# Head mean squares of a hybrid decoder layer: two fp32r matmuls on split squares in place of one fp32 matmul

## The chip, the cores and the metric

One core of one Trainium2 chip runs the kernel. The metric is device time in microseconds (us). Three runs of the kernel before took 942.68, 943.15 and 943.49 us; the median is 943.15.

## What is computed

The reference is one layer of a decoder trunk for 512 prompt rows and 8 sample rows, width 1024. The part that matters here is the RMS norm of each head's output, in the two branches (HGRN2: 8 heads of width 64; retention: 4 heads of width 128):

```python
def _head_rmsnorm(o, n_heads, g):
    b, l, w = o.shape
    oh = o.reshape(b, l, n_heads, w // n_heads)
    oh = oh * lax.rsqrt(jnp.mean(oh * oh, axis=-1, keepdims=True) + EPS)
    return oh.reshape(b, l, w) * g.astype(jnp.float32)

a_hg = _head_rmsnorm(_merge_heads(o_hg), HG_HEADS, g_hg_out) * silu(hg)   # branch A
a_r  = _head_rmsnorm(_merge_heads(o_r), RET_HEADS, g_ret_out) * silu(rg)  # branch B
```

Everything else of the layer (input projection, the two recurrences, the branch and output projections, ConvFFN, per-layer embedding, final norm) is unchanged.

## The kernel before

Activations are kept transposed: channels on the 128 partitions, the 520 rows (512 prompt, 8 sample) along the free dimension. The projections are done in sections named A, V, B, C, D, E, F, G, H. Each section is a run of units; one unit is a stripe of weights of 128 output columns. A unit's raw weights arrive by a DMA on SP's queue (`load`, L396), ScalarE (ACT) makes their high part in the narrow 4-byte kind fp32r (`hi`, L831), VectorE (DVE) the low part (`lo`, L1168), and TensorE (PE) multiplies (`product`, L485): for each 128 channels, high by high, high by low and low by high, each in two halves of 260 columns. There are two weight slots, so the high and low part of unit k+2 are made when the products of unit k are done.

The recurrences run beside the projections, by hand placed into the order of each engine. Both go over the prompt in four chunks of 128 rows.

Section B (`Fori` over four chunks, L597): between the units B0 to B3 of retention's q, k, v and gate, the PE computes one HGRN2 chunk. Its scores go by seven levels (`scores`, L568, matmul L586 and L582), the DVE merges each level's scores into `sfull` (`merge`, L1276), GpSimd (POOL) makes the decayed queries and keys of the levels (`next_level`, L1598 to L1602), ACT pads the queries (`pad_queries`, L922). Then come the chunk's outputs in the PSUM bank `ob` (L617, L622), the state's update in the bank `mb` (L626), half of unit B3, and in `head_squares` the head mean squares: ACT squares `ob` into `sq` (L968), the PE multiplies `sq` by the block constant `blk64` into `mb` (L635), ACT takes the root into `rs` (L970), the DVE inverts it and gates the output (`gate_outputs`, L1289 to L1293). Before L635 the PE also waits until the DVE has added the state's update out of `mb` (L1336).

Section C (`Fori` over four chunks, L652): between the units C0 to C3 the PE computes one retention chunk. ACT squares `ob` at L1021, the PE multiplies by `ones128` at L684 in the middle of unit C2, ACT takes the root at L1023. The DVE adds the state's update out of `mb` at L1369, scales the sample state `rsm` at L1373, and gates.

```python
pe.wait_ge(sq_ready, it + 1)
wait_misc(M_B, 2, it, 4)                    # until L1336 is done
pe.matmul(mb[:], blk64, sq[:], start=True, stop=True).then_inc(misc_full, 1)
```

`sq`, `blk64` and `ones128` are fp32. Such a matmul leaves two records in the profile, one for each of its two passes over the 512 columns.

Of the kernel before, what the change touches and what calls it, by code (L numbers as in the profile page):

```python
# [62 lines left out]
def hybrid_layer(nc, x_prompt, x_sample, state_hgrn, state_ret, state_conv, p_prompt, p_sample,  # L63
# [30 lines left out]
    class Region:  # L94
# [3 lines left out]
        def __call__(self, name, shape, dt=fp):  # L98
# [9 lines left out]
    raw = [r(f"raw{i}", [128, WMAX]) for i in range(2)]  # L108
    whi = [r(f"whi{i}", [128, WMAX], fr) for i in range(2)]
    wlo = [r(f"wlo{i}", [128, WMAX], fr) for i in range(2)]  # L110
    r = Region(33792, 49152)
    NCST = consts.shape[1]
    CST0 = r.at
# [45 lines left out]
    tl = [None] + [r(f"tl{i}", [128, 4, CH >> i]) for i in range(1, LV + 1)]  # L159
    sbd = r("sbd", [128, 4, 128])  # L160
    qz = r("qz", [128, 2, NS])
    sq = r("sq", [128, 512])
    rs = r("rs", [128, 512])
    vb = r("vb", [128, 1024])
    ks8 = r("ks8", [128, 8])
# [20 lines left out]
    zq = [at(f"zq{i}", [128, 4, 2, CH // 2], o)  # L186
          for i, o in enumerate((T0 + 10400, r.at + 2048, r.at - 2048, T0 + 3 * TT * 4))]
    rsm = r("rsm", [128, 8, 128])

    r = Region(G0, 212832)  # L190
    xtok = at("xtok", [128, 5, DM], G1)
# [52 lines left out]
    with ctx:  # L244
        def sem(name):
            return ctx.enter_context(nc.semaphore(name))
# [43 lines left out]
        staged = sem("staged")  # L290
        outer_ready = sem("outer_ready")
        vst_ready = sem("vst_ready")
        sq_ready = sem("sq_ready")
        o_free = sem("o_free")
        a_done = sem("a_done")
# [158 lines left out]
        def _(pe):  # L454
# [142 lines left out]
            with pe.Fori(0, 4) as it:  # L597

                def first_scores():
                    pe.wait_ge(v_taken, it * 2 + 9)  # L600
                    scores(0, it)

                halves(0, it, first_scores)
                scores(1, it)
                halves(1, it, lambda: scores(2, it))
                scores(3, it)
                pe.wait_ge(prep, it * 8 + 8)
                wait_misc(M_B, 0, it, 4)
                for c in range(4):
                    mm = pe.transpose(mb[:, c * 128:(c + 1) * 128], lk[3][:, c, :], ident)  # L610
                mm.then_inc(misc_full, 1)

                product("B", 2, it, 0, 2, C8, 0, xah, xal)

                pe.wait_ge(o_free, it + 1)
                for c in range(4):
                    pe.matmul(ob[:, c * 128:(c + 1) * 128], sbd[:, c, :], lq[3][:, c, :], start=c == 0, stop=False)  # L617
                pe.wait_ge(merged, it * MERGES + (MERGES + 1))
                pe.wait_ge(vst_ready, it + 1)
                wait_misc(M_B, 1, it, 4)  # L620
                for h in range(8):
                    mm = pe.matmul(ob[64 * (h % 2):64 * (h % 2) + 64, (h // 2) * 128:(h // 2 + 1) * 128],  # L622
                                   vst[:, h * 64:(h + 1) * 64], sfull[:, h, :], start=False, stop=h >= 6)
                mm.then_inc(o_ready, 1)
                for h in range(8):
                    mm = pe.matmul(mb[64 * (h % 2):64 * (h % 2) + 64, (h // 2) * 64:(h // 2 + 1) * 64],  # L626
                                   khat[:, h * 64:(h + 1) * 64], vst[:, h * 64:(h + 1) * 64],
                                   start=True, stop=True)
                mm.then_inc(misc_full, 1)

                def head_squares():

                    pe.wait_ge(sq_ready, it + 1)
                    wait_misc(M_B, 2, it, 4)
                    pe.matmul(mb[:], blk64, sq[:], start=True, stop=True).then_inc(misc_full, 1)  # L635
                    pe.wait_ge(acc_free[0], tidx("B", 2, it) + 1)
                    v_transposes()

                halves(3, it, head_squares)

                wait_misc(M_B, 3, it, 4)
                pe.wait_ge(smp_staged, it + 1)
                pe.wait_ge(ss_ready, it + 1)
                taken()
                for b in range(NS):
                    for h2 in range(2):
                        mm = pe.matmul(mb[64 * h2:64 * h2 + 64, b:b + 1], ss[:, b, :], qz[:, h2, b:b + 1],
                                       start=True, stop=True)
                mm.then_inc(misc_full, 1)
            pe.wait_ge(v_taken, 17)  # L650

            with pe.Fori(0, 4) as it:  # L652
                product("C", 0, it, 0, 0, C8, 0, xah, xal)
                pe.wait_ge(staged, it * 2 + 1)
                pe.wait_ge(vst_ready, it + 5)
                wait_level(L_C, 0, it, 2)
                for h in range(4):
                    mm = pe.matmul(level(0)[:, h * 128:(h + 1) * 128], kst[:, h, :], qst[:, h, :],
                                   start=True, stop=True)
                mm.then_inc(lv_full, 1)  # L660
                wait_level(L_C, 1, it, 2)
                for h in range(4):
                    mm = pe.transpose(level(1)[:, h * 128:(h + 1) * 128], kst[:, h, :], ident)
                mm.then_inc(lv_full, 1)
                product("C", 1, it, 1, 1, C8, 0, xah, xal)
                for b in range(2):
                    pe.wait_ge(lv_free[b], it + L_C // 2 + 1)
                pe.wait_ge(o_free, it + 5)
                pe.wait_ge(staged, it * 2 + 2)
                for h in range(4):  # L670
                    out = ob[:, h * 128:(h + 1) * 128]
                    pe.matmul(out, vst[:, h * 128:(h + 1) * 128], prb[:, h, :], start=True, stop=False)
                    mm = pe.matmul(out, rst[:, h, :], qd[:, h, :], start=False, stop=True)
                mm.then_inc(ret_o, 1)
                wait_misc(M_C, 0, it, 4)
                for h in range(4):
                    mm = pe.matmul(mb[:, h * 128:(h + 1) * 128], ktk[:, h * 128:(h + 1) * 128],
                                   vst[:, h * 128:(h + 1) * 128], start=True, stop=True)
                mm.then_inc(misc_full, 1)

                product("C", 2, it, 0, 2, range(4), 0, xah, xal, last=False)
                pe.wait_ge(sq_ready, it + 5)
                wait_misc(M_C, 1, it, 4)
                pe.matmul(mb[:], ones128[:], sq[:], start=True, stop=True).then_inc(misc_full, 1)  # L684
                product("C", 2, it, 0, 2, range(4, 8), 4, xah, xal, first=False, wait_unit=False)
                wait_misc(M_C, 2, it, 4)
                pe.wait_ge(smp_staged, it + 5)
                pe.wait_ge(rsm_ready, it + 1)
                for b in range(NS):
                    mm = pe.matmul(mb[:, b:b + 1], rsm[:, b, :], qs8[:, b:b + 1], start=True, stop=True)  # L690
                mm.then_inc(misc_full, 1)

                product("C", 3, it, 1, 3, range(5), 0, xah, xal, last=False)

                pe.wait_ge(smp_sq, it + 1)
                wait_misc(M_C, 3, it, 4)
                pe.matmul(mb[:, 0:8], blk64, sqs[:, 0:8], start=True, stop=True)
                pe.matmul(mb[:, 8:16], ones128[:], sqs[:, 8:16], start=True, stop=True).then_inc(misc_full, 1)
                product("C", 3, it, 1, 3, range(5, 8), 5, xah, xal, first=False, wait_unit=False)
# [116 lines left out]
        def _(act):  # L816
# [93 lines left out]
            def pad_queries(l, it):  # L910
# [11 lines left out]
                    ins = act.activation(dst, src, ACT.Copy)  # L922
                ins.then_inc(zq_ready, 1)

            act.wait_ge(v_taken, 9)
            act.dma_start(vs_dram[0], v8h[:]).then_inc(vs_stored, 16)
            act.wait_ge(set_up, 7)
# [3 lines left out]
            def hgrn_chunk(it, last=False):  # L931
# [33 lines left out]
                act.dma_start(hg_sample[0].rearrange("b (c two) k v -> (two k) c b v", two=2)[:, it], ss[:])\  # L965
                    .then_inc(ss_stored, 16)
                act.wait_ge(o_ready, it + 1)
                act.activation(sq[:], ob[:], ACT.Square).then_inc(sq_ready, 1)  # L968
                act.wait_ge(misc_full, it * 4 + (M_B + 3))
                act.activation(rs[:], mb[:], ACT.Sqrt, bias=eps[:]).then_inc(misc_free, 1)  # L970
                act.wait_ge(v_full, it * 2 + 10)
# [20 lines left out]
            with act.Fori(0, 4) as it:  # L992
# [8 lines left out]
                for k in range(4):  # L1001
# [16 lines left out]
                                      .broadcast_to([128, NS, 128])).then_inc(vb_loaded, 32)  # L1018
                    if k == 1:
                        act.wait_ge(ret_o, it + 1)  # L1020
                        act.activation(sq[:], ob[:], ACT.Square).then_inc(sq_ready, 1)  # L1021
                        act.wait_ge(misc_full, it * 4 + (M_C + 2))
                        act.activation(rs[:], mb[:], ACT.Sqrt, bias=eps[:]).then_inc(misc_free, 1)  # L1023
                        act.wait_ge(rsm_ready, it + 1)
# [127 lines left out]
        def _(dve):  # L1152
# [134 lines left out]
            def gate_outputs(gate, it, n, per=1):  # L1287
# [4 lines left out]
                dve.wait_ge(o_free, it + (n + 2))  # L1292
                dve.tensor_tensor(m4(ot[:]), m4(ot[:]), chunk(gate, it), MUL).then_inc(a_done, 1)  # L1293

            def branch_lo(t_lo, t_hi, it, n):

                dve.wait_ge(ah_hi, it + (n + 1))
# [2 lines left out]
            with dve.Fori(0, 4) as it:  # L1300
# [33 lines left out]
                for h2 in range(2):  # L1334
                    mine = slice(64 * h2, 64 * h2 + 64)
                    grown = dve.tensor_tensor(state(h2), state(h2),  # L1336
                                              mb[mine, 0:256].rearrange("p (c v) -> p c v", c=4), ADD)
                grown.then_inc(misc_free, 1)
                dve.wait_ge(misc_free, it * 4 + (M_B + 3))
                gate_outputs(ghg, it, 0)  # L1340

# [12 lines left out]
            with dve.Fori(0, 4) as it:  # L1354
# [12 lines left out]
                step(dve.tensor_tensor(rst[:], rst[:], g128.unsqueeze(2).broadcast_to([128, 4, 128]), MUL))  # L1367
                dve.wait_ge(misc_full, it * 4 + (M_C + 1))
                dve.tensor_tensor(rst[:], rst[:], m4(mb[:]), ADD).then_inc(misc_free, 1)  # L1369
                dve.wait_ge(rsm_loaded, it * 16 + 16)  # L1370
                dve.wait_ge(outer_ready, it + 5)
                grown = rsm[:].rearrange("p b v -> p (b v)")
# [400 lines left out]
```

## Time and profile before

| | |
|---|---|
| median of three runs | 943.15 us |
| profiled execution, its own time | 943.24 us |
| its span, first to last instruction | 941.5 us |
| PE busy | 918.6 us, 98% |
| DVE busy | 524.1 us, 56% |
| ACT busy | 388.6 us, 41% |
| POOL busy | 235.7 us, 25% |
| granted clock of TensorE | 0.996 |
| section B's chunk loop | about 121 to 264 us |
| section C's chunk loop | about 264 to 388 us |

The profile is of one execution. A row of the timeline gives the start, the length, the engine, the line, the operation, output and inputs, and how many instructions were merged into it; in brackets stand the engine's idle time before it and what ended it. A queue row (ACTq, SPq) is a DMA's issue. PEld is TensorE's weight load, which overlaps the matmul before.

### The profile page before, as it was taken

Reading aid. Unit: us, or ns where it says so; the run is one execution under the profiler, and the core shown is the slowest. Engines: PE = TensorE matmul, PEld = TensorE weight load, DVE = VectorE, ACT = ScalarE, POOL = GpSimd, SP = SyncE. Lnnn points to the kernel's source line nnn. Section 1 sums busy time; section 2 is a strip of 40 time slices with the busy share of each in tenths; the row PEclk is TensorE's granted clock in tenths of the full one; section 3 lists DMA queues with packets and bytes.
Section 4 is the critical chain, followed back from the end, with each engine's and each line's share of the span. In section 5 each row is a group of like instructions: output and inputs, shape, how many; then the busy total and the mean of one; then the engine's idle time right before and its main releaser. Section 6 shows DMA issues by size and latency. Waiting matters only on the chain. (4 is left out here: it accounts for less than half of the span.)

```text
span 941.5 us, 21025 instructions
## 1 busy us (share of the span) xinstructions
PE 918.6 (98%) x7964; PEld 904.2 (96%) x7964; DVE 524.1 (56%) x612; ACT 388.6 (41%) x518; POOL 235.7 (25%) x289
## 2 busy tenths in 40 slices
PE   7999999999999999999999999999999999999996
PEld 6999989999999999999999999999999999999995
DVE  5432258878655654666566556666655443434643
ACT  6322355465444544423345444444443221223433
POOL 0007057867410101001641111111111031212341
PEclk9999999999999999999999999999999999999998
DMA  6233533323334344533323333333233433332212
GB/s 221 70 90 90 180 92 90 85 71 89 89 112 119 106 125 142 177 116 98 91 68 104 96 91 89 89 89 89 89 89 100 121 93 92 92 90 63 85 56 91
DMA packets 176472, 94.74 MB, mean 101 GB/s; under 512 B 17888, under 2 KB 174960, under 8 KB 176016
## 3 DMA queue, kind: packets, MB, share of 16 engines
q1 hardware_dynamic: 149698, 80.61, 28.8%
q10 hardware_dynamic: 26736, 13.60, 5.1%
q8 instruction: 26, 0.43, 0.2%
q14 instruction: 12, 0.10, 0.0%
HBM read 86.25 MB, written 8.03 MB: 100 GB/s over the span
## 5 line engine op out<-in xcount | busy, mean ns | idle before, releaser
L1168 DVE TENSOR_TENSOR wlo<-raw,whi 128x1024 fp32r<-128x1024 f32 (+2 forms) x132 | 195.8, 1483 | 174.4 <-ACT whi L831 174.4
L831 ACT ACTIVATE whi<-raw 128x1024 fp32r<-128x1024 f32 (+2 forms) x132 | 146.7, 1111 | 353.4 <-PE acc L485 352.0
L485 PE MATMUL acc<-xah,whi 128*128 128x260 f32 x896 | 187.7, 291 | 0.0
L485 PE MATMUL acc<-xah,wlo 128*128 128x260 f32 x896 | 180.8, 283 | 0.0
L485 PE MATMUL acc<-xal,whi 128*128 128x260 f32 x896 | 180.5, 283 | 0.0
L485 PE MATMUL acc<-xbh,whi 128*128 128x260 f32 x816 | 165.3, 284 | 0.8 <-issue 0.8
L485 PE MATMUL acc<-xbh,wlo 128*128 128x260 f32 x816 | 164.4, 283 | 0.0
L485 PE MATMUL acc<-xbl,whi 128*128 128x260 f32 x816 | 164.2, 283 | 0.0
L485 PEld LDWEIGHTS acc<-xah,whi 128*128 128x128 f32 x896 | 138.6, 189 | 3.3 <-issue 1.9
L485 PEld LDWEIGHTS acc<-xal,whi 128*128 128x128 f32 x896 | 138.6, 189 | 0.0
L485 PEld LDWEIGHTS acc<-xah,wlo 128*128 128x128 f32 x896 | 138.4, 189 | 0.0
L485 PEld LDWEIGHTS acc<-xbh,whi 128*128 128x128 f32 x816 | 125.8, 188 | 1.1 <-issue 1.0
L485 PEld LDWEIGHTS acc<-xbh,wlo 128*128 128x128 f32 x816 | 125.8, 188 | 0.0
L485 PEld LDWEIGHTS acc<-xbl,whi 128*128 128x128 f32 x816 | 125.5, 188 | 0.0
L485 PE MATMUL acc<-ach,whi 128*128 128x260 f32 x352 | 71.2, 283 | 0.0
L485 PE MATMUL acc<-ach,wlo 128*128 128x260 f32 x352 | 70.8, 282 | 0.0
L485 PE MATMUL acc<-acl,whi 128*128 128x260 f32 x352 | 70.6, 282 | 0.0
L1670 POOL TENSOR_TENSOR sqt<-hT 128x520 f32 x23 | 35.5, 1543 | 125.6 <-DVE hT L1423 101.3
L1690 POOL TENSOR_TENSOR gg<-gg,cv 128x520 f32<-128x520 f32 x22 | 28.9, 1314 | 118.1 <-DVE gg L1484 115.3
L485 PEld LDWEIGHTS acc<-acl,whi 128*128 128x128 f32 x352 | 54.3, 188 | 0.0
L485 PEld LDWEIGHTS acc<-ach,whi 128*128 128x128 f32 x352 | 54.2, 188 | 0.1
L485 PEld LDWEIGHTS acc<-ach,wlo 128*128 128x128 f32 x352 | 54.2, 188 | 0.0
(286 smaller groups left out, 1194.7 us busy)
## 6 DMA issues: line engine op xcount, KB each, us to landing
raw<-in_w_in SPq DMA_DIRECT2D x96, 256.0 KB, 3.2
raw<-in_w_up SPq DMA_DIRECT2D x88, 256.0 KB, 3.1
raw<-in_w_down SPq DMA_DIRECT2D x16, 384.0 KB, 3.2
raw<-in_w_down SPq DMA_DIRECT2D x16, 320.0 KB, 3.7
raw<-in_w_out SPq DMA_DIRECT2D x16, 256.0 KB, 3.0
raw<-in_w_ple_gate SPq DMA_DIRECT2D x8, 512.0 KB, 3.7
x_transposed<-xstg SPq DMA_DIRECT2D x1, 2080.0 KB, 7.7
hT<-x_transposed ACTq DMA_DIRECT2D x1, 2080.0 KB, 8.3
```

The lines of the kernel that those rows point to most:

```text
L485: mm = pe.matmul(sums[:, b, 0:HT], wt[slot][:, w], xx[:, c, b * HT:(b + 1) * HT], start=first and i == 0 and q == 0, stop=last and i == n ...
L831: act.activation(whi[k % 2][:, 0:n], raw[k % 2][:, 0:n], ACT.Copy).then_inc(hi_ready, 1)
L1168: dve.tensor_tensor(wlo[k % 2][:, 0:n], raw[k % 2][:, 0:n], whi[k % 2][:, 0:n].bitcast(fp), SUB).then_inc(lo_ready, 1)
L1670: step(pool.tensor_tensor(sqt[:], hT[:, j, :], hT[:, j, :], MUL))
L1690: pool.tensor_tensor(gg[:], gg[:], cv[:], MUL).then_inc(act_ready, 1)
```

## The change

The constants `blk64` and `ones128` get copies in the kind fp32r, `blk64r` and `ones128r`, made once by ACT and placed in the part of the first high-weight slot that sections B and C leave unused. After the square, ACT copies `sq` to `sqh` in fp32r (the high part). The DVE then takes `sq - sqh` in place into `sql`, also fp32r (`squares_lo`), right after the state's update. The PE waits for that and does two accumulating fp32r matmuls of 512 columns, on `sqh` and `sql`, in place of the one fp32 matmul. This happens in the four chunks of section B and in the four of section C. The small matmuls on the sample rows' squares (L697, L698) stay as they were.

```diff
@@ tensor, section B, head_squares (L635)
-                    pe.matmul(mb[:], blk64, sq[:], start=True, stop=True).then_inc(misc_full, 1)
+                    pe.wait_ge(sums_ready, 1)
+                    pe.matmul(mb[:], blk64r[:], sqh[:], start=True, stop=False)
+                    pe.matmul(mb[:], blk64r[:], sql[:], start=False, stop=True).then_inc(misc_full, 1)
@@ tensor, section C (L684)
-                pe.matmul(mb[:], ones128[:], sq[:], start=True, stop=True).then_inc(misc_full, 1)
+                pe.matmul(mb[:], ones128r[:], sqh[:], start=True, stop=False)
+                pe.matmul(mb[:], ones128r[:], sql[:], start=False, stop=True).then_inc(misc_full, 1)
@@ scalar, once, ahead of L925
+            act.activation(blk64r[:], blk64, ACT.Copy)
+            act.activation(ones128r[:], ones128[:], ACT.Copy).then_inc(sums_ready, 1)
@@ scalar, section B (L968); section C (L1021) in the same way with it + 5
-                act.activation(sq[:], ob[:], ACT.Square).then_inc(sq_ready, 1)
+                act.activation(sq[:], ob[:], ACT.Square).then_inc(sq_full, 1)
+                act.wait_ge(sq_full, it + 1)
+                taken()
+                act.activation(sqh[:], sq[:], ACT.Copy).then_inc(sq_hi, 1)
@@ vector
+            def squares_lo(it, n):
+                dve.wait_ge(sq_hi, it + (n + 1))
+                dve.tensor_tensor(sql[:], sq[:], sqh[:].bitcast(fp), SUB).then_inc(sq_ready, 1)
@@ vector, section B, after the state's update (L1336)
                 grown.then_inc(misc_free, 1)
+                squares_lo(it, 0)
                 dve.wait_ge(misc_free, it * 4 + (M_B + 3))
@@ vector, section C, after the state's update (L1369)
                 dve.tensor_tensor(rst[:], rst[:], m4(mb[:]), ADD).then_inc(misc_free, 1)
+                squares_lo(it, 4)
                 dve.wait_ge(rsm_loaded, it * 16 + 16)
```

## Rows read from the trace of the kernel before

**Rows 1.** The page: span and busy time.
```profile
span 941.5 us, 21025 instructions
PE 918.6 (98%) x7964; PEld 904.2 (96%) x7964; DVE 524.1 (56%) x612; ACT 388.6 (41%) x518; POOL 235.7 (25%) x289
```

**Rows 2.** Waits of PE: line, releaser, total us, times, longest.
```profile
PE lvb L586 <- DVE sfull L1276: 2.1, 3, 0.8
```

**Rows 3.** The tile `sq`: its matmuls, duration ns min/median/max, first and last start.
```profile
L635 PE MATMUL mb<-sq,cst x8: 592/593/697, 152.0 to 259.0; 128*128 128x512 f32 x8
L684 PE MATMUL mb<-sq,ones x8: 591/592/592, 282.4 to 373.1; 128*128 128x512 f32 x8
```

**Rows 4.** Timeline of PEld in section C, around L684: start, length.
```profile
282.30 0.31 PEld L684 LDWEIGHTS mb<-sq,ones 128*128 128x128 f32 x2
282.85 0.19 PEld L485 LDWEIGHTS acc<-xah,whi 128*128 128x128 f32 x1 [0.24 <-issue]
283.27 0.19 PEld L485 LDWEIGHTS acc<-xah,whi 128*128 128x128 f32 x1 [0.24 <-issue]
283.40 0.31 PEld L485 LDWEIGHTS acc<-xal,whi 128*128 128x128 f32 x2
```

**Rows 5.** Timeline in section C, first chunk: ACT's square, DVE's steps.
```profile
278.85 0.60 ACT L1021 ACTIVATE sq<-ob 128x512 f32<-128x512 f32 x1 [0.23 <-PE ob L673]
280.11 0.69 DVE L1369 TENSOR_TENSOR rst<-rst,mb 128x512 f32<-128x512 f32 x1
280.71 1.28 DVE L1373 SCALAR_TENSOR_TENSOR rsm<-rsm,cst,vb 128x1024 f32<-128x1024 f32 x1
286.05 1.87 PEld L690 LDWEIGHTS mb<-qs,rsm 128*128 128x128 f32 x16
```

**Rows 6.** Single lines of DVE: duration ns min/median/max.
```profile
L1367 DVE TENSOR_TENSOR rst<-rst,cst x4: 678/686/689, 279.3 to 369.6; 128x512 f32<-128x512 f32 x4
L1168 DVE TENSOR_TENSOR wlo<-raw,whi x132: 1215/1226/2376, 17.9 to 914.8; 128x1024 fp32r<-128x1024 f32 x108, 128x1408 fp32r<-128x1408 f32 x16, 128x1280 fp32r<-128x1280 f32 x8
```

**Rows 7.** Timeline in section B, first chunk: before L635.
```profile
148.49 0.60 ACT L968 ACTIVATE sq<-ob 128x512 f32<-128x512 f32 x1 [0.37 <-PE ob L622]
151.09 0.85 DVE L1336 TENSOR_TENSOR sbd<-sbd,mb 64x256 f32<-64x256 f32 x2
152.00 0.30 PEld L635 LDWEIGHTS mb<-sq,cst 128*128 128x128 f32 x2 [0.35 <-DVE sbd L1336]
```

**Rows 8.** Timeline in section B, first chunk: POOL beside DVE.
```profile
147.25 1.30 POOL L1601 TENSOR_TENSOR lk<-lk,fT 128x256 f32<-128x256 f32 x1
147.76 1.87 DVE L1168 TENSOR_TENSOR wlo<-raw,whi 128x1024 fp32r<-128x1024 f32 x1
151.93 0.73 POOL L1601 TENSOR_TENSOR lk<-lk,tl 128x256 f32<-128x256 f32 x1
```

**Rows 9.** Timeline in section B, from the root to the next chunk's second scores.
```profile
153.16 0.69 ACT L970 ACTIVATE rs<-mb,eps 128x512 f32<-128x512 f32 x1 [2.77 <-PE mb L635]
154.41 3.50 ACT L922 ACTIVATE zq<-lq 64x256 f32<-64x256 f32 x8
157.94 1.06 ACT L831 ACTIVATE whi<-raw 128x1024 fp32r<-128x1024 f32 x1
160.31 0.60 ACT L982 ACTIVATE sg<-acc 128x520 f32<-128x520 f32 x1
161.09 0.76 DVE L1345 SCALAR_TENSOR_TENSOR grt<-acc,vc,sg 128x520 f32 x1 [0.84 <-ACT sg L982]
164.16 1.31 DVE L1276 COPY_PREDICATED sfull<-msk,lvb 128x512 f32<-128x512 uint32 x1 [0.15 <-DVE sfull L1276]
165.62 1.15 PE L586 MATMUL lvb<-zq,lk 128*64 128x64 f32 x32 [0.78 <-DVE sfull L1276]
```

**Rows 10.** Timeline in section B, last chunk.
```profile
256.50 0.85 DVE L1336 TENSOR_TENSOR sbd<-sbd,mb 64x256 f32<-64x256 f32 x2
258.55 1.02 PE L635 MATMUL mb<-sq,cst 128*128 128x512 f32 x2
```

**Rows 11.** Timeline of ACT where section B begins.
```profile
122.47 0.25 ACT L899 ACTIVATE v8h<-lvb 8x128 f32 x1
123.47 2.20 ACT L922 ACTIVATE zq<-lq 64x256 f32<-64x256 f32 x5 [0.76 <-ACT v8h L899]
```

More of the change, by code:

```diff
@@ L110, in hybrid_layer @@
     wlo = [r(f"wlo{i}", [128, WMAX], fr) for i in range(2)]
+    blk64r = at("blk64r", [128, 128], 2 * WMAX * 4 + 1024 * 4, fr)
+    ones128r = at("ones128r", [128, 128], 2 * WMAX * 4 + 1152 * 4, fr)
     r = Region(33792, 49152)
@@ L161, in hybrid_layer @@
     qz = r("qz", [128, 2, NS])
+    SQ0 = r.at
     sq = r("sq", [128, 512])
+    sql = at("sql", [128, 512], SQ0, fr)
     rs = r("rs", [128, 512])
@@ L188, in hybrid_layer @@
     rsm = r("rsm", [128, 8, 128])
+    sqh = r("sqh", [128, 512], fr)
     r = Region(G0, 212832)
@@ L292, in hybrid_layer @@
         vst_ready = sem("vst_ready")
+        sums_ready = sem("sums_ready")
+        sq_full = sem("sq_full")
+        sq_hi = sem("sq_hi")
         sq_ready = sem("sq_ready")
@@ L1020, in _ @@
                         act.wait_ge(ret_o, it + 1)
-                        act.activation(sq[:], ob[:], ACT.Square).then_inc(sq_ready, 1)
+                        act.activation(sq[:], ob[:], ACT.Square).then_inc(sq_full, 1)
+                        act.wait_ge(sq_full, it + 5)
+                        taken()
+                        act.activation(sqh[:], sq[:], ACT.Copy).then_inc(sq_hi, 1)
                         act.wait_ge(misc_full, it * 4 + (M_C + 2))
```

## The prediction

> **What bounds the kernel now.** I read the page first: PE is busy 918.6 of 941.5 us [rows 1], and every other engine has half its time free or more. So what shortens PE's own work is worth its full length, and what lengthens another engine's work costs something only where PE waits for that engine. The second view is PE's list of waits, cut to sections B and C: in C nothing that the head squares touch makes it wait, but in B it waits three times, once at each passage from one chunk to the next, for the DVE's merge [rows 2]. The third view is the timeline around L635 and L684. Here the reader is to see who comes last. At L684 (section C) the PE runs on without a gap. At L635 (section B, first chunk) its weight load stands 0.35 us idle until the DVE's state update, L1336, has ended [rows 7]; chunks 1 and 2 show the same picture 35.7 and 71.3 us later, the last chunk doesn't [rows 10]. So the same edit meets two situations: five of the eight places bound by PE, three held by the DVE.
>
> **PE's part.** The fp32 matmul of 512 columns leaves two records of 592 ns [rows 3], but records overlap, so I take the spacing of the weight loads. Around L684 the loads of the next product start at 282.85 and 283.27, 0.42 to 0.43 us apart, against 0.12 between two loads of a fp32r product of 260 columns (0.31 less the 0.19 of one) [rows 4]. From L684's first load at 282.30 to the load at 283.40 are four spacings and 1.10 us, two of them of 0.12: the two passes take 0.86 together. The two new matmuls are of the product's kind, with 512 columns. By columns one takes 0.12 x 512 / 260 = 0.24; if part of the 0.12 is fixed, about 0.22. I take 0.23, so the pair 0.46 and the saving 0.40 at each place. No row shows this kind at 512 columns: the bounds are 0 (it takes as long as a fp32 pass) and 0.42 (two of 0.22).
>
> **ACT's copy to sqh.** The nearest row is the square, 0.60 [rows 5, 7]. In B it starts at 149.1, where ACT next has a table load and then 2.77 us idle until the PE has finished [rows 7, 9]; in C the idle is 2.73. It ends at 149.7 (B) and 280.1 (C), before the DVE comes to its part (151.9 and 280.7). It costs nothing; the cover is those 2.7 us, and if it were gone it would be 0.6 on each of eight places.
>
> **DVE's squares_lo in C.** A tensor_tensor of 512 columns with both inputs in SBUF takes 0.69 (L1367) [rows 6]. It follows L1369, which ends at 280.80; DVE instructions overlap by 0.09 (L1373 starts at 280.71) [rows 5], so it runs from 280.71 to 281.40. The PE wants it at 282.30 [rows 4]: 0.9 us of cover. Behind it L1373 slips by 0.6, to an end at 282.6, and the reader of `rsm` is L690 at 286.05 [rows 5], so that is covered too; the store of `rsm` on ACT's queue stands behind the root at 283.5 anyway. The other three chunks have the same distances within 0.2. All of PE's gain stays: 4 x -0.40 = -1.60 us. Downstream of it is the inversion of 3.35, which waits for the root and so comes earlier with the PE.
>
> **DVE's squares_lo in B, chunks 0 to 2.** Here the PE already waits for L1336 [rows 7], and now for what stands behind it. L1336 ends at 151.94; squares_lo starts about 0.08 before, lasts 0.69, and releases the PE some 0.06 later, as L1336 did: 152.62 in place of 152.00. POOL's L1600 holds on to 151.93, which may add a few hundredths. I take +0.65. Behind the waiting matmul are queued the value transposes and the second half of B3; all of PE shifts by 0.65 - 0.40 = +0.25. The second path: ACT's root comes 1.16 after the first weight load now (152.00 to 153.16 [rows 7, 9]) and 0.43 to 0.40 sooner after it then, so it too starts +0.25 later. From there ACT goes on without a gap (value copies, eight query copies of 3.50, the weights' high part, a table load, the sigmoid at 160.31), the DVE takes over at 161.09 after 0.84 idle for that sigmoid, merges, and releases the PE at 165.62 after 0.78 idle [rows 9]. The idle before that matmul can't absorb the +0.25, since its releaser hangs from the same root and slips as much. The three places give 3 x +0.25 = +0.75.
>
> **B, last chunk.** L1336 ends at 257.35 and the PE comes at 258.55 [rows 10]; squares_lo ends at about 257.96 and is covered by 0.6. The gain stays: -0.40.
>
> **The two constants.** ACT copies 128 columns twice, once, between L899 and the DMA issue ahead of the padded queries. A copy of 128 columns is a record of 0.25 (L899), and ACT has 0.76 idle there, in which its queue only issues that DMA [rows 11]. The PE's first scores wait for the queries, so this is on the path: 0 if the copies run during the issue, 0.45 at most if the issue waits for them. I take 0, since no wait stands between the copies and the issue other than that for L899.
>
> **Sum.** -1.60 + 0.75 - 0.40 + 0 = -1.25 us. The profiled execution took 943.24 us (its span of 941.5 and 1.74 around it), 0.09 above the median of three. It gives 943.24 - 1.25 = 941.99, say 942.0: 0.12% below the median. A measurement of this kernel can tell about 0.2% from no change, which is 1.89 us around 943.15, or 941.26 to 945.04. The forecast is no measurable difference.
>
> **A rule that speaks against it.** The row: L1168 starts at 147.76 while POOL's L1601 runs until 148.55, and takes 1.87 us against its usual 1.23, 0.64 more [rows 6, 8]. The DVE seems to stand until POOL's instruction is over. The Trainium skill (SBUF — State Buffer, Who interferes with whom) says that a DVE instruction with two SBUF inputs and a GpSimd instruction that reads SBUF exclude each other for a whole instruction, and that issue order decides. By that rule, the trace agrees. `squares_lo` has two SBUF inputs where L1336 has one. This gives the first rival.
>
> **Rival 1: POOL gets there first.** In chunks 0 to 2 POOL's next instruction, L1601, starts at 151.93 and takes 0.73 [rows 8]; squares_lo would be ready at 151.86. With 0.07 us between them either may win. If POOL wins, squares_lo ends some 0.7 later and the PE with it: 3 x 0.7 = +2.1, so 944.1, a small loss but still within 0.2%. For it: the closeness. Against it: the DVE would already be standing when POOL's L1600 ends, as L1168 was at 148.5 when it got its turn ahead of POOL's next. Chance 0.15.
>
> **Rival 2, the other side: the pair isn't short.** If one fp32r matmul of 512 columns takes as long as one fp32 pass, 0.43, the saving is gone at all eight places and the three delays of 0.65 stay: +1.95, so 945.2, slower by 0.2%. The place is L635 in chunks 0 to 2; the change is a loss from the point where the saving is under 1.95 / 8 = 0.24, that is where the pair takes over 0.62. For it: no row has this kind at 512 columns, and none has an accumulating pair into `mb`. Against it: thousands of products of 260 columns go at 0.12. Chance 0.05. Copies of the constants that aren't hidden would come on top, to 945.6.
>
> **Rival 3: the delay in B is absorbed.** If the merge that releases L586 hangs from POOL or from the next chunk's level data rather than from the root, the 0.78 us idle [rows 9] swallows the 0.25 three times: -2.05 + 0, so 941.2, at the edge of measurably faster. For it: waits are put down to the last releaser alone. Against it: ACT's gapless run from 153.16 to 160.91. Chance 0.12.
>
> **How the numbers follow.** Forecast 0.62 with its own range 941.4 to 942.8 (saving 0.38 to 0.42, delay 0.6 to 0.8); rival 1 0.15 at 944.1; rival 2 0.05 at 945.2; rival 3 0.12 at 941.2; 0.06 for what none names. The range runs from 941.0 to 944.3. Faster by over 0.2%: half of rival 3 and a little of the rest, 0.09. Slower by over 0.2%: rival 2 and a little of the rest, 0.08. Within: 0.83.
>
> **What would show it.** Right, if the weight loads around L684 stand about 0.23 apart; if L684's section loses 0.4 us a chunk; if the idle before L635 in chunks 0 to 2 grows from 0.35 to about 1.0 with squares_lo as releaser, and squares_lo lasts about 0.7; if the root starts 0.25 later relative to L1336; if the idle before L586 stays near 0.78. Rival 1 shows as squares_lo of 1.4 us in B; rival 2 as spacings of 0.43; rival 3 as an idle before L586 under 0.6. What would make the prediction wrong is a shift of POOL and DVE against each other in B, which changes the contended merges behind it, by some tenths in each chunk.

## The result and the profile after

The changed kernel takes 943.73 us against 942.63 before (medians of 20 runs each); the ratio is 1.0014 with a 95% interval of 1.0007 to 1.0020. So it is slower, by about 1.1 to 1.3 us: under the 0.2% that was named as the bound of what can be told, but with 20 runs of each the interval leaves out 1. The forecast was 942.0, 1.2 us under its reference, so a change with the other sign. Every ratio in this document is of undisturbed executions; one of the eleven of the kernel with both repairs took 2284 us and is left out of its ratio.

The page of the changed kernel, its first rows (compare [rows 1]), and under them PE's waits in total us, times and longest (compare [rows 2]):

```profile
span 943.4 us, 21059 instructions
PE 914.6 (97%) x7964; PEld 903.6 (96%) x7964; DVE 531.0 (56%) x620; ACT 394.5 (42%) x528; POOL 237.5 (25%) x289
...
PE mb L645 <- DVE sql L1318: 4.7, 3, 1.6
...
PE lvb L595 <- DVE sfull L1296: 2.3, 3, 0.8
```

PE is busy 4 us less, and a new wait stands at the top of its list: 4.7 us, three times, for `squares_lo` (L1318). The wait for the merge (L1296, L1276 before) is still there with 2.3 us. Both halves of the forecast's picture are to be seen: less work, and a longer wait in three places.

The span alone misleads. Its difference, 1.9 us, holds 0.6 us from the start of the kernel, where the PE waits for loads that land at other times from trace to trace (its first matmul, released by the constants' DMA, starts at 3.51 before and at 3.98 after): the transposes ahead of section B start at 120.34 before and 120.94 after. What doesn't depend on the start is the period from one chunk of B to the next. I read it off the state's matmuls (`mb<-vst,khat`), start of the first in each chunk, PE's timeline of the changed kernel:

```profile
148.82 0.64 PE L635 MATMUL mb<-vst,khat 128*64 128x64 f32 x16
185.50 0.64 PE L635 MATMUL mb<-vst,khat 128*64 128x64 f32 x16
222.20 0.63 PE L635 MATMUL mb<-vst,khat 128*64 128x64 f32 x16
258.91 0.63 PE L635 MATMUL mb<-vst,khat 128*64 128x64 f32 x16
```

The kernel before, the same:

```profile
148.18 0.64 PE L626 MATMUL mb<-vst,khat 128*64 128x64 f32 x16
183.91 0.63 PE L626 MATMUL mb<-vst,khat 128*64 128x64 f32 x16
219.50 0.63 PE L626 MATMUL mb<-vst,khat 128*64 128x64 f32 x16
254.98 0.64 PE L626 MATMUL mb<-vst,khat 128*64 128x64 f32 x16
```

The periods are 35.73, 35.59 and 35.48 before and 36.68, 36.70 and 36.71 after: 106.80 against 110.09 in all, +3.29 us. The sample's small matmuls after the last chunk's head squares start 3.53 later than before (266.45 against 262.92) where the state's matmuls started 3.93 later: -0.40 in the last chunk. In section C the saving is four times 0.40 (below); the first weight loads of its head squares come every 30.09 or 30.10 us before and every 29.68 after. That gives +3.29 - 0.40 - 1.60 = +1.3 us, as the runs say.

Now the place itself, changed kernel, first chunk of B, the timeline of all engines without the products (compare [rows 7, 8]):

```profile
151.73 0.85 DVE L1361 TENSOR_TENSOR sbd<-sbd,mb 64x256 f32<-64x256 f32 x2
151.85 0.74 POOL L1627 TENSOR_TENSOR lq<-lq,tl 128x256 f32<-128x256 f32 x1
...
152.56 0.74 POOL L1628 TENSOR_TENSOR lk<-lk,tl 128x256 f32<-128x256 f32 x1
152.61 1.22 DVE L1318 TENSOR_TENSOR sql<-sq,sqh 128x512 fp32r<-128x512 f32 x1
153.25 0.85 POOL L1629 TENSOR_TENSOR tl<-tl 128x128 f32<-128x128 f32 x1
154.05 0.19 PEld L645 LDWEIGHTS mb<-sqh,blk64r 128*128 128x128 f32 x1 [1.77 <-issue]
154.08 0.47 PE L645 MATMUL mb<-sqh,blk64r 128*128 128x512 f32 x1 [1.58 <-DVE sql L1318]
154.16 0.19 PEld L646 LDWEIGHTS mb<-sql,blk64r 128*128 128x128 f32 x1
...
154.82 0.69 ACT L987 ACTIVATE rs<-mb,eps 128x512 f32<-128x512 f32 x1 [3.02 <-PE mb L646]
```

From the end of the state update (L1361, 152.58) to the first weight load (154.05) are 1.47 us. Before it was 0.06. The reader can take it apart: `squares_lo` starts 0.03 after the update's end; it lasts 1.22, where in C it lasts 0.68 or 0.69; and it ends at 153.83, 0.22 ahead of the weight load. POOL's L1628 started at 152.56, 0.05 before `squares_lo`. Against that the root comes 0.77 after the first weight load, where it was 1.16, a saving of 0.39. 1.47 - 0.06 - 0.39 = +1.02 a chunk, three times +3.06 of the +3.29.

In B's last chunk no POOL instruction runs at this place, and the same instruction, with the same two SBUF inputs, takes 0.69:

```profile
260.42 0.85 DVE L1361 TENSOR_TENSOR sbd<-sbd,mb 64x256 f32<-64x256 f32 x2
261.30 0.69 DVE L1318 TENSOR_TENSOR sql<-sq,sqh 128x512 fp32r<-128x512 f32 x1
262.35 0.19 PEld L645 LDWEIGHTS mb<-sqh,blk64r 128*128 128x128 f32 x1
```

Section C, weight loads around the head squares in the changed kernel (compare [rows 4]):

```profile
285.83 0.19 PEld L695 LDWEIGHTS mb<-sqh,ones128r 128*128 128x128 f32 x1
285.95 0.19 PEld L696 LDWEIGHTS mb<-sql,ones128r 128*128 128x128 f32 x1
286.19 0.41 PEld L494 LDWEIGHTS acc<-xah,whi 128*128 128x128 f32 x2
286.53 0.31 PEld L494 LDWEIGHTS acc<-xal,whi 128*128 128x128 f32 x2
```

Four spacings take 0.70 (285.83 to 286.53) where they took 1.10: the saving is 0.40, and one narrow matmul of 512 columns takes about 0.23.

### The profile page after: what moved, and what is told of

Same layout as the page of the kernel before. It is cut to its first block and busy times, and to the rows that moved or that the text cites. A ratio compares the mean times of both kernels' runs of the same rounds, so it can differ in the third digit from the quotient of the medians.

```text
span 943.4 us, 21059 instructions
## 1 busy us (share of the span) xinstructions
PE 914.6 (97%) x7964; PEld 903.6 (96%) x7964; DVE 531.0 (56%) x620; ACT 394.5 (42%) x528; POOL 237.5 (25%) x289
```

## The experiments

The theory that the result suggested: the pair saves 0.40 at all eight places; the loss is all in B's chunks 0 to 2, in the path state update, `squares_lo`, matmul, root, merge, second scores. It has three parts: the step's own length, POOL in front of it, and a late release. The rivals stand in each expectation. Each kernel ran 5 to 11 times; ratios are to the kernel before, run on the same chip. "Period" is always the time from the first of the state's matmuls in one chunk of B to that in the next.

### Section C alone, section B alone

```diff
 e1_c_only (section B as in the kernel before; waits and their counts left out)
-                act.activation(sq[:], ob[:], ACT.Square).then_inc(sq_full, 1)
-                act.activation(sqh[:], sq[:], ACT.Copy).then_inc(sq_hi, 1)
+                act.activation(sq[:], ob[:], ACT.Square).then_inc(sq_ready, 1)
-                squares_lo(it, 0)
-                    pe.matmul(mb[:], blk64r[:], sqh[:], start=True, stop=False)
-                    pe.matmul(mb[:], blk64r[:], sql[:], start=False, stop=True).then_inc(misc_full, 1)
+                    pe.matmul(mb[:], blk64, sq[:], start=True, stop=True).then_inc(misc_full, 1)
 e2_b_only: the same three edits in section C instead, with ones128
```

> Section B as before, the narrow pair in section C alone. Theory (the pair saves 0.40 us wherever the PE bounds, the loss sits in B's DVE step): 4 x -0.40 = -1.6 us against before, ratio 0.9983, and the passages between B's chunks as before. Rival (the pair or the setup costs something outside B too, such as the start of the kernel, which was 0.6 us later in the changed kernel's trace): no better than before, ratio 1.000.

> The narrow pair in section B alone, section C as before. Theory: chunks 0 to 2 cost +1.0 us each, the last gains 0.4: +2.6 to +2.9 us against before, ratio 1.003, and the sum of this and the C-only kernel's difference is that of the whole change (+1.1). Rival (loss outside B): under +1.5.

Measured: C alone 0.9989 (0.9980 to 0.9998), so faster by 1.0 us, 1.2 by the medians (941.05 against 942.22), where -1.6 was expected; B alone 1.0033 (1.0020 to 1.0045), +3.1 us, where +2.6 to +2.9 was expected. The periods in B are 35.74, 35.64 and 35.59 in the first, as before, and 36.42 to 36.44 in the second. Both rivals fall: the part in C is a gain and the part in B a loss. The sum, +2.1 us, lies above the whole change's 1.3, by less than the intervals leave open.

The traces say where the 3.1 us of B alone lie, and they are not all in B. The periods give 3 x 0.83 - 0.40 = +2.1. Another 1.1 us lie behind 929.7, in the last 14 us of this one trace, where the granted clock reads 0.74 from 930 to 935 and 0.98 in the changed kernel's trace. From the first of the state's matmuls to the end of the span C alone takes 1.6 us less than the kernel before (791.7 for 793.3), which is the expectation.

The period of B alone, 36.43, is also 0.27 under the changed kernel's 36.70, with the same code in B. The difference is a second meeting of DVE and POOL, at the low part of the gated output (`ahl`, L1298 before, two SBUF inputs), on the path from the root to the merge. Changed kernel, and under it B alone, first passage of each:

```profile
163.47 0.40 POOL L1626 COPY lk<-lk 128x256 f32<-128x256 f32 x1
163.50 0.90 DVE L1323 TENSOR_TENSOR ahl<-ot,ahh 128x512 f32 x1
...
161.69 0.68 DVE L1319 TENSOR_TENSOR ahl<-ot,ahh 128x512 f32 x1
161.75 0.88 POOL L1621 COPY lk<-lk 128x256 f32<-128x256 f32 x1
```

Where POOL comes first by 0.03, the DVE takes 0.90; where the DVE comes first by 0.06, it takes 0.68 and POOL 0.88. All three passages of B alone go the DVE's way and all three of the changed kernel go POOL's way; the PE then waits about 0.5 and about 0.8 us for the merge. In the kernel before the first two passages go POOL's way (0.92, 0.89) and the third the DVE's way (0.68, with POOL held to 0.95, their starts 0.01 apart; wait 0.53).

### The order of the PE's waits

```diff
-                    pe.wait_ge(sq_ready, it + 1)
                     wait_misc(M_B, 2, it, 4)
                     pe.wait_ge(sums_ready, 1)
+                    pe.wait_ge(sq_ready, it + 1)
```

> The changed kernel with the PE's wait for sq_ready in B moved behind its two other waits. Of the 1.41 us from the end of the state update to the first weight load 0.22 lie between the end of squares_lo and that load, against 0.06 before, when the last wait was the one that ended last. Theory W (the PE has two more wait instructions to pass after the late one): the 0.22 falls to 0.06, 3 x -0.16 = -0.5 us against the changed kernel. Rival (the longer release belongs to the DVE's write or to the start of the narrow matmul): stays 0.22, no change.

Measured: ratio 1.0006 (0.9997 to 1.0015); the periods are 36.52, 36.57 and 36.56, so 0.14 a chunk less than the changed kernel's 36.70. First chunk, timeline:

```profile
150.63 1.23 DVE L1318 TENSOR_TENSOR sql<-sq,sqh 128x512 fp32r<-128x512 f32 x1
...
151.98 0.19 PEld L645 LDWEIGHTS mb<-sqh,blk64r 128*128 128x128 f32 x1 [1.57 <-issue]
```

`squares_lo` ends at 151.86 and the load stands at 151.98: 0.12 in place of 0.22. (The distance from the update's end to the load in the changed kernel is 1.47; the 1.41 of the expectation is what it grew by.) So theory W holds for 0.10 of the 0.16. The rest of the distance to 0.06 belongs to neither of the two waits, and stays open.

### The squares in an idle PSUM bank

```diff
-                act.activation(sq[:], ob[:], ACT.Square).then_inc(sq_full, 1)
+                act.activation(lvb[:, 1, :], ob[:], ACT.Square).then_inc(sq_full, 1)
-                act.activation(sqh[:], sq[:], ACT.Copy).then_inc(sq_hi, 1)
+                act.activation(sqh[:], lvb[:, 1, :], ACT.Copy).then_inc(sq_hi, 1)
-                dve.tensor_tensor(sql[:], sq[:], sqh[:].bitcast(fp), SUB).then_inc(sq_ready, 1)
+                dve.tensor_tensor(sql[:], lvb[:, 1, :], sqh[:].bitcast(fp), SUB).then_inc(sq_ready, 1)   # in B
```

> The changed kernel with the squares of section B in an idle PSUM bank instead of SBUF, so that squares_lo has one SBUF input. Theory L (squares_lo stands 0.53 us because POOL's instruction holds what both need for a second SBUF input): squares_lo takes 0.69 instead of 1.22, and the kernel gains 3 x 0.53 = 1.6 us on the changed kernel, to about 0.5 under before. Rival (the 1.22 is the instruction itself in this place, such as reading what ACT has just written): stays 1.2, no gain.

Measured: ratio 0.9992 (0.9983 to 1.0001), periods 36.01, 36.09 and 36.10. First chunk, timeline:

```profile
150.85 0.85 DVE L1361 TENSOR_TENSOR sbd<-sbd,mb 64x256 f32<-64x256 f32 x2
...
151.67 0.74 POOL L1628 TENSOR_TENSOR lk<-lk,tl 128x256 f32<-128x256 f32 x1
151.73 0.69 DVE L1318 TENSOR_TENSOR sql<-lvb,sqh 128x512 fp32r<-128x512 f32 x1
152.37 0.40 POOL L1629 TENSOR_TENSOR tl<-tl 128x128 f32<-128x128 f32 x1
152.64 0.19 PEld L645 LDWEIGHTS mb<-sqh,blk64r 128*128 128x128 f32 x1 [1.24 <-DVE sbd L1361]
```

The period falls by 0.61 to 0.67. The two instructions meet in the same way (151.67 and 151.73), POOL's runs its 0.74 as before, but the DVE's now runs beside it in 0.69, and POOL's next one takes 0.40, not 0.85. One SBUF input less is all that changed for the DVE, so theory L holds: 0.53 us of the 1.22 were a stand behind POOL. That the same two SBUF inputs take 0.69 in the last chunk, without POOL, says the same. The rule of the Trainium skill cited with the prediction (SBUF — State Buffer, Who interferes with whom) describes this; by that rule, the trace agrees in both directions, blocked with two SBUF inputs and free with one.

### Both together

The edits of the two kernels before this one, in one.

> The changed kernel with both repairs: squares of B in the idle PSUM bank, and the wait for sq_ready last of the PE's waits. If the two parts add, the period from chunk to chunk in B, 36.70 us in the changed kernel, falls by 0.60 to 0.65 for the bank (as in that kernel alone) and by 0.13 for the order of the waits, to 35.9; that is about the +0.25 a chunk over the kernel before that was forecast for the change itself. The time: 1.3 us under before, ratio 0.9986. Rival (they don't add, since another releaser stands close behind): period 36.05, ratio 0.9992.

Measured: ratio 0.9991 (0.9981 to 1.0001), periods 36.08, 36.05 and 36.03. The rival's numbers came. First chunk, timeline:

```profile
149.40 0.85 DVE L1361 TENSOR_TENSOR sbd<-sbd,mb 64x256 f32<-64x256 f32 x2
...
150.28 0.69 DVE L1318 TENSOR_TENSOR sql<-lvb,sqh 128x512 fp32r<-128x512 f32 x1
...
151.09 0.19 PEld L645 LDWEIGHTS mb<-sqh,blk64r 128*128 128x128 f32 x1 [1.06 <-DVE sbd L1361]
...
151.87 0.69 ACT L987 ACTIVATE rs<-mb,eps 128x512 f32<-128x512 f32 x1 [2.46 <-PE mb L646]
```

The release is again 0.12 (150.97 to 151.09), yet the period isn't shorter. PE's wait for `squares_lo` fell from 3.1 us in the bank's kernel to 2.6 here, and its wait for the merge rose from 2.0 to 2.3. So the tenth was gained and given back on the way to the merge: the root starts 5.35 behind the state's matmul, where it was 5.44 to 5.49 in the bank's kernel. From the root to the next chunk's matmul are 30.68 to 30.73, where the bank's kernel had 30.52 once, in the one passage in which its DVE came ahead of POOL at `ahl` (0.68), and 30.64 and 30.65 in the others. The first passage thus loses 0.21 there in the second meeting; the 0.03 and 0.06 of the other two have no named step. The kernel also says what the change costs a chunk with both mishaps gone: 0.84 from the update's end to the load, less the 0.06 of before and less 0.38 at the root (0.78 in place of 1.16), is +0.40, and 36.05 - 35.60 = +0.45 is measured.

### The head squares later in unit B3

```diff
-                halves(3, it, head_squares)
+                product("B", 3, it, 1, 3, range(6), 0, xah, xal, last=False)
+                head_squares()
+                product("B", 3, it, 1, 3, range(6, 8), 6, xah, xal, first=False, wait_unit=False)
```

> The changed kernel with the head squares of B after six of the eight steps of unit B3 instead of four, so that the PE comes to them 1.4 us later, about when squares_lo is done. Theory R (the price is paid on the path root, ACT, merge, second scores, which hangs from squares_lo): the idle before the head squares falls from 1.58 us to about 0.2, the idle before the next chunk's second scores grows from 0.79 to about 2.2, and the time is that of the changed kernel within 0.5 us, ratio to before 1.001. Rival P (the price is the PE's own idle at the head squares): 3 x 1.3 = 3.9 us faster than the changed kernel, ratio to before 0.997.

Measured: ratio 1.0041 (1.0028 to 1.0055), slower than either theory said. The periods tell why: 36.49 in the first passage, but 38.05 and 38.03 in the second and third. PE's wait for the merge is now 6.2 us in three, and the granted clock of TensorE in stretches around the second passage reads (columns: us, busy time of each engine, PEclk, DMA share, GB/s):

```profile
200.00:202.00 2.00, 0.44 (x4) 0.23 (x2) 1.85 (x2) 1.42 (x2) 1.95 (x5) 1.00 0.73 178
202.00:204.00 2.00, 1.47 (x32) 1.47 (x32) 0.84 (x2) 1.92 (x5) 0.66 (x3) 0.75 0.41 97
204.00:206.00 2.00, 2.00 (x12) 1.91 (x10) 1.85 (x3) 0.58 (x2) 2.00 (x4) 0.50 0.15 34
206.00:208.00 2.00, 2.00 (x17) 2.00 (x16) 1.87 (x4) 0.83 (x2) 1.76 (x4) 0.90 0.09 24
```

The second scores wait 2.09 us there, and behind that wait, from 203 until past 206, the clock stands at 0.50, its 1.2 GHz level; the scores take 1.63 us instead of 1.15. The third passage shows 0.63 and 0.51 at 240 to 244. In the first passage the wait was 2.03 and the clock stayed at 1.00. The first passage is therefore the one that tells the two theories apart. Against the changed kernel its period is 36.49 for 36.68. The idle before the head squares has gone (1.58 to 0.27 at the weight load), and the idle before the second scores is 2.03 for 0.79. The root starts 5.99, 6.03 and 6.02 behind the state's matmul, in the changed kernel 6.00, 6.02 and 6.02: the path didn't move. Theory R holds and rival P, which wanted a period of 35.4, falls: what the PE doesn't wait at the head squares it waits at the merge. The other two passages are longer by 1.35 us than in the changed kernel and by 1.55 than the first one here; the low clock stands in these two alone, but no trace gives one of them at the high clock, so its price is inferred. One of the five runs, at a mean clock of 0.994, took 944.12 us, the other four 946.26 to 946.87. With twice 1.35 taken off, the time is within 0.5 us of the changed kernel's, as theory R said.

### The low part of B left out

```diff
-                squares_lo(it, 0)
-                    pe.wait_ge(sq_ready, it + 1)
+                    pe.wait_ge(sums_ready, 1)
+                    pe.wait_ge(sq_hi, it + 1)
                     wait_misc(M_B, 2, it, 4)
-                    pe.wait_ge(sums_ready, 1)
                     pe.matmul(mb[:], blk64r[:], sqh[:], start=True, stop=False)
-                    pe.matmul(mb[:], blk64r[:], sql[:], start=False, stop=True).then_inc(misc_full, 1)
+                    pe.matmul(mb[:], blk64r[:], sqh[:], start=False, stop=True).then_inc(misc_full, 1)
```

> The changed kernel without squares_lo in section B: the low part is left out there, and both narrow matmuls of B multiply the high part (so the means of B are not the reference's). Theory (the whole loss is the DVE step in the path, the narrow pair itself saves 0.40 at all eight places): the first weight load stands 0.1 behind the state update, the root 0.75 behind that, 8 x -0.40 = -3.2 us against before, ratio 0.9966. Rival (narrow pair, constants or ACT's copy cost something in B): above 0.998.

Measured: ratio 0.9967 (0.9955 to 0.9979), expected 0.9966. Periods 35.27, 35.24 and 35.22. The state update ends at 151.44 in the first chunk, and:

```profile
151.49 0.19 PEld L645 LDWEIGHTS mb<-sqh,blk64r 128*128 128x128 f32 x1 [0.35 <-DVE sbd L1361]
...
152.26 0.69 ACT L987 ACTIVATE rs<-mb,eps 128x512 f32<-128x512 f32 x1 [1.61 <-PE mb L646]
```

The load is 0.05 behind the update as in the kernel before, with the same idle of 0.35, and the root 0.77 behind the load. So the narrow pair, the constants and ACT's copy cost nothing in B: the DVE step in the path, with its slower release, is the whole loss. (The wait that ends last stands last here, as in the kernel before, so this kernel is also free of the late release.)

### The head squares in a bank of their own

```diff
 both kernels:
+                    matmuls of the head squares write lvb[:, 1, :], not mb; ACT's root reads it there
-                    wait_misc(M_B, 2, it, 4)
                 wait_misc(M_B, 3, it, 4)
+                pe.transpose(lvb[0:NS, 1, 0:128], hiT[:, NT:TT], ident).then_inc(v_full, 1)   # was in head_squares
+                    ACT's copy of it to v8r stands behind the padded queries, not ahead of them
 e8_own_bank also, on the vector engine, order in B:
+                squares_lo(it, 0)
                 for h2 in range(2):
                     step(dve.tensor_tensor(state(h2), state(h2), tl[LV][mine].broadcast_to([64, 4, 64]), MUL))
...
                 grown.then_inc(misc_free, 1)
-                squares_lo(it, 0)
 e9_own_bank_fp32: fp32 matmul in B as before, narrow pair in C alone
```

> A version meant to keep the change's gain: in B the narrow pair goes to an idle PSUM bank instead of mb, so the PE needn't wait for the state update, and the DVE does squares_lo ahead of the state update, in the time in which the PE does its half unit; the small transpose of the sample rows moves behind the root. Theory R: the root starts 0.3 (no wait for the state update) and 0.4 (the pair) earlier than in the kernel before, in three chunks 3 x -0.7, last chunk -0.4, section C 4 x -0.4: -4.1 us, ratio 0.9957. Rival (the moved state update is late for someone, or POOL's instructions block the DVE in the new place): above 0.998.

> The same bank and the same moved transpose, but with the fp32 matmul in B as before (narrow pair in C alone). It tells how much of the own-bank version comes from the bank: theory -0.35 in three chunks and -1.6 in C, -2.6 us against before, ratio 0.9972, so 1.5 us slower than the narrow own-bank version. Rival (in B the narrow kind gives nothing even so): equal to the narrow one within 0.3 us.

Measured: the narrow one 0.9965 (0.9953 to 0.9977), 938.49 against 942.16 us, so faster than both kernels; the fp32 one 0.9981 (0.9972 to 0.9990). The periods are 34.93, 34.88 and 34.93 against 35.23, 35.27 and 35.26, and 35.60 before in the mean: the bank gives 0.35 a chunk, the narrow pair another 0.34, the -0.7 of the expectation. ACT's copy of the sample values, which moved in both kernels, gave nothing to see: from the root to the next chunk's matmul both need 30.65 to 30.74 us, the kernel before 30.49 to 30.75. The narrow one's first chunk:

```profile
148.56 0.69 DVE L1320 TENSOR_TENSOR sql<-sq,sqh 128x512 fp32r<-128x512 f32 x1 [0.34 <-ACT sqh L987]
...
150.24 0.19 PEld L644 LDWEIGHTS lvb<-sqh,blk64r 128*128 128x128 f32 x1
...
150.49 0.85 DVE L1364 TENSOR_TENSOR sbd<-sbd,mb 64x256 f32<-64x256 f32 x2
...
151.02 0.69 ACT L989 ACTIVATE rs<-lvb,eps 128x512 f32<-128x512 f32 x1 [1.28 <-PE lvb L645]
```

`squares_lo` ends 1.0 us ahead of the load, and the PE has no idle before it; the state update is done later and nobody on the path waits for it. By ratios the two gain 3.3 and 1.8 us where 4.1 and 2.6 were expected. The traces show that nothing is missing behind the start: from the first of the state's matmuls to the end of the span are 793.3 us before, 789.2 in the narrow kernel and 790.6 in the fp32 one, so -4.1 and -2.8. What the ratios lack lies ahead of that point, where the start comes at other times from trace to trace, or in the interval of each ratio, about 1 us to either side.

## Why the prediction was wrong

The time lies inside the range, but the change has the other sign. That the range holds it isn't luck either: it was drawn out to rival 1, which came true. Rival 1 put the changed kernel 0.85 us above the kernel before (944.1 for 943.24); measured are 1.1 to 1.3. Step by step:

- **The pair.** Forecast 0.46 for two and 0.40 saved; measured 0.40 in C, 0.39 at the root in B. Right. Rival 2, the pair that isn't short, is dead.
- **ACT's copy and the two constants.** Forecast 0. ACT's padded queries start 0.76 after the end of the sample values' copy, as before (123.32 to 124.08), with both constants made in between; and the kernel with the high part twice shows B free of cost without the DVE step. Right.
- **C, and B's last chunk.** Forecast 4 x -0.40 and -0.40 with 0.9 and 0.6 us of cover. Measured -0.40 in the spacing and 3.93 to 3.53 in the last chunk; `squares_lo` ends 0.90 ahead of the load in C and 0.36 ahead in B's last chunk. Right; by its runs C's share is 1.0 to 1.2 us, by its trace 1.6.
- **B, chunks 0 to 2.** Forecast +0.65 at the matmul and +0.25 net; measured +1.41 and +1.0. This is the step that failed: the term `squares_lo` in the path was put at +0.65 and measured +1.41. Its three parts: the stand behind POOL, 0.53, which was rival 1 at a price of 0.7 and got 0.15 of the chance; the start, 0.03 after the update's end and not 0.08 before it, 0.11; the release, 0.22 and not 0.06, 0.16. Together 0.80; the measured 1.02 - 0.25 = 0.77 bears that out to 0.03.
- **Where the choice went wrong.** The forecast put `squares_lo` at 151.86 and POOL's L1601 at 151.93 [rows 8] and gave the DVE the turn. The 0.08 of overlap was taken from L1369 and L1373 in section C; behind the state update in B it doesn't exist, neither in the changed kernel nor with the source in PSUM (151.70 to 151.73), nor in the last chunk, where POOL is away (261.27 to 261.30). The DVE came 0.05 after POOL in place of 0.07 ahead, in each of the three chunks. A race decided by 0.07 us, with a borrowed overlap in it, deserved near even chances and not 0.15. Why the overlap is absent there wasn't tested. One difference stands in the rows: the update's second half lies on partitions 64 to 127 and `squares_lo` starts at partition 0, while in the narrow own-bank kernel the update's first half, which starts at partition 0 too, comes behind `squares_lo` with 0.08 of overlap (149.25 to 149.17).
- **The path.** Forecast: the delay goes root, ACT, merge, second scores and isn't absorbed by the 0.78 idle. The idle is 0.79 in the changed kernel, and the kernel with the later head squares shows that the PE's own idle isn't the price. Right, and rival 3 is dead. One thing was missed: before, the third passage had an idle of 0.53 only; now it is 0.77, +0.24 once. It is the second meeting of DVE and POOL, at `ahl`, which the DVE had won there before and loses now; the last line of the prediction had named such a shift.
- **Without the mishaps** the step would still have cost +0.45 a chunk, not +0.25, as the kernel with both repairs shows. Then the change gains by 3 x 0.45 - 2.0 = -0.65 us, in keeping with its ratio of 0.9991, whose interval just includes 1.
- **Small slips, which change no term.** The DVE is busy 56% of the span, so it has less than half its time free. Rival 3's -2.05 is -2.00 by its own terms (-1.60 - 0.40).

## What to carry to other kernels

A cheaper matmul is worth its price only where PE comes last; where it already waits for the engine that must now do one more step, that step counts in full, with its stand behind another engine's instruction and with its release. Before putting a step between a releaser and its waiter, look for a place ahead of the releaser and a bank of its own for the result: the change that lost 1 us a chunk gained 0.7 there, 0.35 by the bank and 0.34 by the narrow pair. When two engines' instructions start within 0.1 us of each other on the path, price both orders. And in a kernel whose start jitters by a microsecond, compare periods of its loops, not spans.

## What the runs showed of the hardware

- A DVE tensor_tensor with both inputs in SBUF that starts 0.05 us behind a POOL tensor_tensor takes 1.22 us instead of 0.69; with one input in PSUM, in the same place, it takes 0.69, and POOL's next instruction takes 0.40 instead of 0.85.
- The order decides who is held: at `ahl` the DVE takes 0.90 and POOL 0.40 with POOL 0.03 ahead, and the DVE takes 0.68 and POOL 0.88 with the DVE 0.06 ahead.
- The release of a waiting PE took 0.22 us when two more, already satisfied waits stood behind the late one, and 0.12 when the late one was last.
- An idle of 2.09 us on the PE and one of 2.07 were each followed by a granted clock of 0.50 (1.2 GHz) for over 2 us, in passages 1.35 to 1.55 us longer; an idle of 2.03 at the first passage was not followed by one. Idles of 1.6 and 0.8 in one chunk, as in the changed kernel, left the clock at 1.00.
- By the spacing of the weight loads, the fp32 matmul of 512 columns takes 0.86 us of the PE, a fp32r one 0.23.
